# GpSimd only subtracts, ScalarE makes the first parts of its weight pieces, and two small chains of VectorE stand earlier

## The chip, the cores and the metric

The kernel runs on one core of a Trainium2 chip. Its time is the device time of one execution in microseconds (us), here the median of three. The engines of the core are named as in the profile: PE is TensorE (PEld its weight loads), DVE is VectorE, ACT is ScalarE, POOL is GpSimd, and SP issues the loads from HBM. Each engine works through its own list of instructions in order; they meet only in semaphores.

## The reference

Two transformer blocks run one after the other on 256 tokens of width 1024, all in float32. The second block is the one that the change touches: its input projection makes the queries, keys and values of a gated delta rule, of a compressed, a selected and a windowed attention, and the gates of both.

```
def first_block(...):           # three attentions, then a gated FFN
    h = h + concat([y_a, y_b, y_c]) @ w_out
    h = h + (silu(hn @ w_gate) * (hn @ w_up)) @ w_down
    return rms_norm(h, final_norm)[:, META_BLK:]

def second_block(x, ...):
    h = rmsnorm(x, norm_mix)
    (dn_qkv, dn_z, dn_b, dn_a, ns_q, ns_kc, ..., ns_gate, gate_dn, gate_nsa) = split(h @ w_in)
    o_dn = gated_deltanet(dn_qkv, dn_z, dn_b, dn_a, dn_conv, dn_a_log, dn_dt_bias, dn_out_norm)
    o_ns = nsa_mixer(...)
    mix = sigmoid(gate_dn) * (o_dn @ w_proj_dn) + sigmoid(gate_nsa) * (o_ns @ w_proj_nsa)
    x = x + mix @ w_out
    return x + square(relu(rmsnorm(x) @ w_up)) @ w_down

def gated_deltanet(qkv, z, b_logit, a_logit, ...):
    q, k, v = split(silu(causal_depthwise_conv(qkv, conv_w)))
    q, k = l2norm(q), l2norm(k)
    beta = sigmoid(b_logit)
    g = -exp(a_log) * softplus(a_logit + dt_bias)
    o = chunk_gated_delta_rule(q, k, v, g, beta)
    return rmsnorm(o, out_norm) * silu(z)
```

## The kernel before

**Weight pieces.** All weights come in some 250 pieces, most of 128 partitions by 1024 float32 numbers (512 KB), in the fixed order of the list `PIECES`. SP loads piece i into slot i modulo 5 of `raw`, as soon as the second part of piece i-5 is made. Each piece is then split into two parts of a faster matrix format, in slot i modulo 6 of `parts`: the first part is a rounded copy, the second is what is left (piece minus first part). A product on PE takes three matmuls: first by first, first by second, second by first (lines 529 to 531).

**Who splits.** For most pieces ACT makes the first part (`first_parts`, line 1302) and DVE the second (`second_parts`, line 1814). Twenty pieces, `dv1`, `dq0`, `dq1`, `z0` and `z1` (four each), are in `BY_POOL`: POOL makes both parts in `pool_parts`, a cast (line 1753) and a subtraction (line 1755). ACT and DVE come to their splits through `full`, `freed` and `beyond`: before they wait for a product of PE they split the four pieces that follow the ones that this product used. POOL has no such rule: it takes the next piece when it is loaded and the slot in `parts` is free.

**The join.** Where the second block's projections go over into its attention (`attention(G2, ...)`), each engine's order is written by hand. DVE does the four-tap convolutions of the keys (`convolve("k", 0, 4, 0)`, then `("k", 0, 4, 1)`, the jobs `cv_k2` and `cv_k3`) and of the first values (`EARLY`, the job `cv_v0`), each seven or eight reads of a PSUM bank and a last read (line 2213) that gives the bank back. Then it scales the residual X by its norm and gain (`inv_sqrt`, 11 dependent instructions in lines 1838 to 1846, and two of line 2265), makes the gates (lines 2268 to 2274), and takes the peaks of the first attention groups (`peaks_of`, line 1891). ACT makes exponentials from the peaks (line 1344), PE turns these (line 610 or 624).

**In the attention.** There are 24 groups (compressed, selected and windowed, each for four heads). Between them seven "fillers" stand at groups 0, 1, 3, 4, 7, 10 and 13 (`FILL`): PE makes a product of two pieces, DVE convolves it. Filler 0 uses `dv0.2` and `dv0.3`, filler 1 `dv1.0` and `dv1.1`, and so on to `dq1.3`. At groups 15, 17, 19 and 21 ACT makes decays (line 1613).

**After the attention.** POOL masks the four tiles of decays (line 1765) and scales them by the keys' norms (line 1772). ACT applies SiLU to the convolutions (line 1555). PE does the product of `z0`, turns, the products `qk` and `kk` (line 1120), and then the product of `z1`. The banks for the product of `z1` are the first two of `qk` and `kk`, which DVE gives back in lines 2404 and 2406, after it has made the queries' norms (`inv_rms`, lines 1838 to 1854).

Of the kernel before, what the change touches and what calls it, by code (L numbers as in the profile page):

```python
# [150 lines left out]
def build(nc, consts, params, weights, x, meta, out, line_dram):  # L151
    ctx = ExitStack()
    with ctx:
# [5 lines left out]
        def sem(name):  # L159
            if name not in sems:  # L160
                sems[name] = ctx.enter_context(nc.semaphore(name))
            return sems[name]
# [132 lines left out]
        def signal(ins, name, by=1):  # L295

            ins.then_inc(sem(name), by)
            counts[name] = counts.get(name, 0) + by
            return counts[name]
# [12 lines left out]
        def loaded(eng, name):  # L312

            i = INDEX[name]
            eng.wait_ge(sem(f"piece_in{i % RAW}"), 16 * (i // RAW + 1))
            return raw[:, i % RAW, 0:WIDTHS[name]]

        def split_slot(name):

            if name in APART:  # L320
                apart = arena_r[:, apart_at[APART.index(name)]:][:, 0:2 * PIECE]
                return apart[:, 0:PIECE], apart[:, PIECE:2 * PIECE]
            j = PART[name] % SPLIT
            return parts[:, j, 0, 0:WIDTHS[name]], parts[:, j, 1, 0:WIDTHS[name]]

        def slot_free(eng, name):

            if name not in APART and PART[name] >= SPLIT:
                used_up(eng, RING[PART[name] - SPLIT])
# [954 lines left out]
        def _(act):  # L1284
# [9 lines left out]
            def first_parts(n):  # L1294

                for name in PIECES[at[0]:n]:
                    at[0] += 1
                    if name in WHOLE or name in BY_POOL:
                        continue
                    whole_piece = loaded(act, name)  # L1300
                    slot_free(act, name)
                    signal(A(split_slot(name)[0], whole_piece, ACT.Copy), "first_parts")  # L1302

            keep_ahead[act] = first_parts

# [413 lines left out]
        @block.gpsimd  # L1719
        def _(pool):  # L1720
            nc.gpsimd.memset(ones[:, :], 1.0).then_inc(sem("ones"), 1)
            nc.gpsimd.memset(att1["PTm"], 0.0).then_inc(sem("meta_zero"), 1)
            nc.gpsimd.memset(one["V"][:, 0:768], 0.0).then_inc(sem("meta_zero"), 1)
            nc.gpsimd.memset(VC[:, :, :], 0.0).then_inc(sem("vc_zero"), 1)
            nc.gpsimd.memset(kcT[:, :, :], 0.0).then_inc(sem("kc_zero"), 1)

            pool.wait_ge(sem("lines_out"), 16)

            def shifted(head0, heads, v, m0, n):
                return bass.AP(tensor=line_dram.tensor, offset=head0 * 2 * LINE + v * LINE + m0,  # L1730
                               ap=[[1, P], [2 * LINE, heads], [1, n]])

            sz0 = one["sz0"].rearrange("p (h n) -> p h n", h=SH)
            sz1 = one["sz1"].rearrange("p (h n) -> p h n", h=SH)
            pool.dma_start(one["dz"].rearrange("p (h n) -> p h n", h=DH), shifted(0, DH, 0, 0, ALL)).then_inc(sem("dz_in"), 16)
            pool.dma_start(sz0[:, :, 0:META], shifted(DH, SH, 0, P, META)).then_inc(sem("sz_in"), 16)
            pool.dma_start(sz0[:, :, META:144], shifted(DH, SH, 1, P + META, P)).then_inc(sem("sz_in"), 16)
            pool.dma_start(sz1[:, :, 0:META], shifted(DH, SH, 0, 0, META)).then_inc(sem("sz_in"), 16)
            pool.dma_start(sz1[:, :, META:ALL], shifted(DH, SH, 1, META, SEQ)).then_inc(sem("sz_in"), 16)

            pool.wait_ge(sem("norm3"), 2)
            al = nsa["alibi"].rearrange("p (h n) -> p h n", h=NSH)
            for h in range(NSH):
                slope = float(np.float32(2.0 ** (-8.0 * (h + 1) / NSH)))
                nc.gpsimd.tensor_scalar(al[:, h, :], cst("negdist"), slope, None, ALU.mult).then_inc(sem("alibi"), 1)  # L1745

            def pool_parts(names):

                for name in names:
                    whole_piece = loaded(pool, name)  # L1750
                    slot_free(pool, name)
                    first, second = split_slot(name)
                    nc.gpsimd.tensor_copy(first, whole_piece).then_inc(sem("pool_first"), 1)
                    pool.wait_ge(sem("pool_first"), TURN[name])
                    nc.gpsimd.tensor_tensor(second, whole_piece, first.bitcast(F32), ALU.subtract)\  # L1755
                        .then_inc(sem("split_pool"), 1)

            by_pool = [name for name in PARTED if name in BY_POOL]
            pool_parts(by_pool[:-2])

            E4 = dn["DT"].rearrange("p (g n) -> p g n", g=4)
            for g in range(4):
                pool.wait_ge(sem("dec_exp"), g + 1)
                v = E4[:, g, :].rearrange("p (n i) -> p n i", n=GH)
                nc.gpsimd.tensor_tensor(v, v, cst("upper").unsqueeze(1).to_broadcast([P, GH, P]), ALU.mult)\
                    .then_inc(sem("dec_masked"), 1)
            pool.wait_ge(sem("key_scale"), 1)
            for g in range(4):
                pool.wait_ge(sem("dec_masked"), g + 1)
                v = E4[:, g, :].rearrange("p (n i) -> p n i", n=GH)  # L1770
                k2 = st[:, 112 + GH * g:116 + GH * g].unsqueeze(2).to_broadcast([P, GH, P])
                nc.gpsimd.tensor_tensor(v, v, k2, ALU.mult).then_inc(sem("dec_scaled"), 1)
            pool_parts(by_pool[-2:])

            pool.wait_ge(sem("split_pool"), len(by_pool))
            pool.wait_ge(sem("y_new"), 1)
            nc.gpsimd.memset(dn["Yi"].rearrange("p (g n) -> p g n", g=2 * GH * TT)[HB:P, :, 0:HB], 0.0).then_inc(sem("y_zero"), 1)

            for j in range(FT2 // 2):
                v = relu2[:, j % 4, :]  # L1780
                pool.wait_ge(sem("hidden2_first"), j + 1)
                nc.gpsimd.tensor_tensor(v, v, v, ALU.mult).then_inc(sem("squares2"), 1)  # L1782
                pool.wait_ge(sem("squares2"), j + 1)
                nc.gpsimd.tensor_tensor(a2[:, 1, 2 * j:2 * j + 2, :], v, a2[:, 0, 2 * j:2 * j + 2, :].bitcast(F32), ALU.subtract)\
                    .then_inc(sem("hidden2"), 1)
# [3 lines left out]
        def _(dve):  # L1789
# [403 lines left out]
            def convolve(which, w, first, n):  # L2193

                name = f"cv_{which}{first // 2 + n}"
                full(dve, name)
                both = [(first + 2 * n + j, bank_of(name)[:, SEQ * j:SEQ * j + SEQ]) for j in range(2)]
                for h, raw in both:
                    step(V_.tensor_scalar(cv[:, w, h, :], raw, taps[:, 8 * w + h, 3:4], None, ALU.mult))
                settle()  # L2200
                for back in (1, 2, 3):
                    for h, raw in both:
                        o = cv[:, w, h, back:SEQ]
                        ins = V_.scalar_tensor_tensor(out=o, in0=raw[:, 0:SEQ - back], scalar=taps[:, 8 * w + h, 3 - back:4 - back],
                                                      in1=o, op0=ALU.mult, op1=ALU.add)
                        if back < 3:
                            step(ins)
                        else:
                            signal(ins, "conv_raw")
                    if back < 3:  # L2210
                        settle()

                release(V_.tensor_copy(scr[:, 512 + n:513 + n], bank_of(name)[:, 0:1]), name)  # L2213
# [42 lines left out]
            for t in range(TT):  # L2256
                v = nsa["ksw"][:, 512 * t:512 * t + 512].rearrange("p (h d) -> p h d", d=ND)
                signal(V_.tensor_tensor(v, v, bc(st[:, 80 + 8 * t:88 + 8 * t], [P, 8, ND]), ALU.mult), "nk_norm")
            convolve("k", 0, 4, 0)
            convolve("k", 0, 4, 1)  # L2260
            for what in EARLY:
                convolve(*what)
            inv_sqrt(st[:, 4:6], st[:, 30:32], st[:, 0:2], st[:, 24:26])
            for t in range(TT):
                signal(V_.scalar_tensor_tensor(out=X[:, t, :], in0=X[:, t, :], scalar=st[:, 4 + t:5 + t], in1=att1["final"],
                                               op0=ALU.mult, op1=ALU.mult), "x2")
            dve.wait_ge(sem("small_ln"), 1)
            link(V_.tensor_scalar(sig[:, :], sig[:, :], 1.0, None, ALU.add))
            link(V_.reciprocal(sig[:, :], sig[:, :]))
# [3 lines left out]
            link(V_.tensor_scalar(soft[:, 48:56], soft[:, 48:56], -1.0, None, ALU.mult))  # L2273
            signal(V_.tensor_tensor(gl[:, :, :], soft[:, 0:16].rearrange("p (t h) -> p t h", t=TT),
                                    soft[:, 48:56].unsqueeze(1).to_broadcast([P, TT, NH2]), ALU.mult), "gates")

            def finish_two(g):

                c0 = g["first"]
# [401 lines left out]
```

## Time and profile before

| what | value |
|---|---|
| median of 3 runs | 962.51 us (961.49 to 962.91) |
| the profiled execution's own time | 962.28 us |
| its span, first to last instruction | 960.4 us |
| PE busy | 915.4 us, 95% |
| DVE busy | 630.2 us, 66% |
| ACT busy | 465.3 us, 48% |
| POOL busy | 156.2 us, 16% |
| PE idle at the join | 13.1 us, in one wait |
| mean granted clock of PE | 0.991 |

A profile row has its start in us, how long it took, the engine, the line of the kernel, the instruction, and what it writes and reads. "x4" joins four alike in a row. In brackets stands how long the engine was idle just before, and who released it. PEclk is the clock granted to PE as a share of 2.4 GHz, so 0.50 is 1.2 GHz.

### The profile page before, as it was taken

How to read it: one execution, taken by the hardware profiler on the slowest of the kernel's cores; microseconds unless marked ns; L12 is line 12 of the kernel's file. 1: busy time of each engine (PE TensorE's matmuls, PEld its weight loads, DVE VectorE, ACT ScalarE, POOL GpSimd, SP SyncE). 2: the span in 40 equal slices, each digit the busy share in tenths (PEclk: the TensorE clock that was granted, in tenths of full speed). 3: DMA queues.
4: the chain of work that ended last, by engine and by line, in shares of the span. 5: the costliest groups of instructions: out<-in, count | busy, mean ns of one | idle time of the engine just before them, and what ended most of it. 6: DMA issues, size and time to landing. Idle time of an engine off the chain costs nothing. (4 is left out here: it accounts for less than half of the span.)

```text
span 960.4 us, 17495 instructions
## 1 busy us (share of the span) xinstructions
PE 915.4 (95%) x6858; PEld 818.7 (85%) x6858; DVE 630.2 (66%) x1338; ACT 465.3 (48%) x925; POOL 156.2 (16%) x111
## 2 busy tenths in 40 slices
PE   4999899999999999999499999999999999999998
PEld 1988687999999989889488898898888889999996
DVE  4556776656556678697787977545966666445543
ACT  6554555545344463564134575354454454454441
POOL 2000000000000015005475314000000023233221
PEclk9999999999999999999799999999999999999999
DMA  8530244565556445646232202022455546555551
GB/s 303 177 135 23 88 133 130 158 216 182 171 195 220 155 143 176 219 160 203 77 114 86 67 1 78 3 70 88 164 187 178 186 153 218 186 176 176 184 189 44
DMA packets 38679, 139.61 MB, mean 145 GB/s; under 512 B 4331, under 2 KB 4587, under 8 KB 38597
## 3 DMA queue, kind: packets, MB, share of 16 engines
q1 hardware_dynamic: 37184, 134.17, 42.3%
q10 hardware_dynamic: 884, 2.49, 0.8%
q0 software_dynamic: 528, 1.84, 0.6%
q8 instruction: 55, 0.90, 0.4%
q14 instruction: 28, 0.22, 0.1%
HBM read 137.39 MB, written 1.08 MB: 144 GB/s over the span
## 5 line engine op out<-in xcount | busy, mean ns | idle before, releaser
L1814 DVE TENSOR_TENSOR parts<-raw,parts 128x1024 fp32r<-128x1024 f32 (+2 forms) x225 | 286.8, 1310 | 138.6 <-ACT parts L1302 134.1
L1302 ACT ACTIVATE parts<-raw 128x1024 fp32r<-128x1024 f32 (+2 forms) x225 | 228.0, 1050 | 119.2 <-PE psum L531 97.7
L529 PE MATMUL psum<-hT,parts 128*128 128x256 f32 (+1 forms) x928 | 264.7, 285 | 2.3 <-DVE hT L1831 2.0
L530 PE MATMUL psum<-hT,parts 128*128 128x256 f32 (+1 forms) x928 | 263.4, 284 | 0.0
L531 PE MATMUL psum<-hT,parts 128*128 128x256 f32 (+1 forms) x928 | 261.7, 282 | 0.0
L529 PEld LDWEIGHTS psum<-hT,parts 128*128 128x128 f32 x928 | 175.7, 189 | 5.6 <-DVE hT L1831 2.9
L531 PEld LDWEIGHTS psum<-hT,parts 128*128 128x128 f32 x928 | 176.9, 191 | 0.0
L530 PEld LDWEIGHTS psum<-hT,parts 128*128 128x128 f32 x928 | 176.0, 190 | 0.6
L529 PE MATMUL psum<-parts,arena_r 128*128 128x512 f32 x344 | 135.1, 393 | 0.9 <-DVE arena_r L1829 0.7
L531 PE MATMUL psum<-parts,arena_r 128*128 128x512 f32 x344 | 134.0, 389 | 0.0
L530 PE MATMUL psum<-parts,arena_r 128*128 128x512 f32 x344 | 133.9, 389 | 0.0
L1344 ACT ACTIVATE arena<-arena,npeaks 128x128 f32<-128x128 f32 (+4 forms) x136 | 55.9, 414 | 66.5 <-DVE npeaks L1913 51.3
L529 PEld LDWEIGHTS psum<-parts,arena_r 128*128 128x128 f32 x344 | 64.6, 188 | 14.6 <-DVE arena_r L1829 1.8
L531 PEld LDWEIGHTS psum<-parts,arena_r 128*128 128x128 f32 x344 | 64.6, 188 | 13.6
L530 PEld LDWEIGHTS psum<-parts,arena_r 128*128 128x128 f32 x344 | 64.6, 188 | 12.6
L529 PE MATMUL psum<-parts,hT 128*128 128x512 f32 (+1 forms) x176 | 69.7, 396 | 1.7 <-DVE peaks L1891 1.1
L1745 POOL TENSOR_SCALAR arena<-cbuf 128x256 f32<-128x256 f32 x16 | 16.8, 1050 | 333.8 <-DVE scr L2131 332.7
L530 PE MATMUL psum<-parts,hT 128*128 128x512 f32 (+1 forms) x176 | 68.8, 391 | 0.0
L531 PE MATMUL psum<-parts,hT 128*128 128x512 f32 (+1 forms) x176 | 68.7, 390 | 0.0
L1782 POOL TENSOR_TENSOR arena<-arena 128x512 f32<-128x512 f32 x16 | 17.2, 1075 | 284.7 <-ACT arena_r L1715 284.7
L1755 POOL TENSOR_TENSOR parts<-raw,parts 128x1024 fp32r<-128x1024 f32 x20 | 48.4, 2418 | 1.6
L652 PE MATMUL psum<-arena 128*128 128x128 f32 x288 | 40.2, 276 | 2.1 <-DVE scr L2213 1.2
(324 smaller groups left out, 1184.5 us busy)
## 6 DMA issues: line engine op xcount, KB each, us to landing
raw<-weights SPq DMA_DIRECT2D x247, 512.0 KB, 4.1
raw<-weights SPq DMA_DIRECT2D x4, 384.0 KB, 7.4
X<-x SPq DMA_DIRECT2D x2, 512.0 KB, 6.1
out<-X SPq DMA_DIRECT2D x2, 512.0 KB, 2.6
arena<-lines POOLq DMA_DIRECT2D x1, 768.0 KB, 9.7
cbuf<-consts ACTq DMA_DIRECT2D x1, 561.0 KB, 5.1
arena<-lines POOLq DMA_DIRECT2D x1, 544.0 KB, 7.8
arena<-params ACTq DMA_DIRECT2D x1, 512.0 KB, 8.9
```

Of the source, the lines that this page charges most:

```text
L529: mm(ps, a, c, start=start, stop=False)
L530: mm(ps, a, d, start=False, stop=False)
L531: return mm(ps, b, c, start=False, stop=stop)
L652: last = mm(o, flat[:, at:at + P], vt[t], start=(t == 0 and not g["meta"]), stop=(t == g["tiles"] - 1))
L1302: signal(A(split_slot(name)[0], whole_piece, ACT.Copy), "first_parts")
L1344: signal(A(map_slot(g, E, n), map_slot(g, S, n), ACT.Exp, bias=npeaks[:, col:col + 1], accum_out=sums[:, col:col + 1]), tag)
L1745: nc.gpsimd.tensor_scalar(al[:, h, :], cst("negdist"), slope, None, ALU.mult).then_inc(sem("alibi"), 1)
L1755: nc.gpsimd.tensor_tensor(second, whole_piece, first.bitcast(F32), ALU.subtract)\
L1782: nc.gpsimd.tensor_tensor(v, v, v, ALU.mult).then_inc(sem("squares2"), 1)
L1814: signal(V_.tensor_tensor(second, whole_piece, first.bitcast(F32), ALU.subtract), "split_vector")
```

## The change

Three things change.

POOL's cast is gone. For the twenty pieces of `BY_POOL`, ACT now makes the first part too, in its usual `first_parts`, and signals `first_for_pool`; POOL waits for that and only subtracts. ACT's place for it is that of every other piece: up to four pieces ahead of the last product that it has come to.

The gates (five instructions) move ahead of the convolution `cv_k2`.

The residual's norm and scaling (13 instructions) move ahead of the convolution `cv_k3`, behind an explicit call that makes the second parts due there.

```diff
                 for name in PIECES[at[0]:n]:
                     at[0] += 1
-                    if name in WHOLE or name in BY_POOL:
+                    if name in WHOLE:
                         continue
                     whole_piece = loaded(act, name)
                     slot_free(act, name)
-                    signal(A(split_slot(name)[0], whole_piece, ACT.Copy), "first_parts")
+                    signal(A(split_slot(name)[0], whole_piece, ACT.Copy), "first_for_pool" if name in BY_POOL else "first_parts")
...
             def pool_parts(names):
 
                 for name in names:
+                    first, second = split_slot(name)
+                    pool.wait_ge(sem("first_for_pool"), TURN[name])
                     whole_piece = loaded(pool, name)
-                    slot_free(pool, name)
-                    first, second = split_slot(name)
-                    nc.gpsimd.tensor_copy(first, whole_piece).then_inc(sem("pool_first"), 1)
-                    pool.wait_ge(sem("pool_first"), TURN[name])
                     nc.gpsimd.tensor_tensor(second, whole_piece, first.bitcast(F32), ALU.subtract)\
                         .then_inc(sem("split_pool"), 1)
...
-            convolve("k", 0, 4, 0)
-            convolve("k", 0, 4, 1)
-            for what in EARLY:
-                convolve(*what)
-            inv_sqrt(st[:, 4:6], st[:, 30:32], st[:, 0:2], st[:, 24:26])
-            for t in range(TT):
-                signal(V_.scalar_tensor_tensor(out=X[:, t, :], in0=X[:, t, :], scalar=st[:, 4 + t:5 + t], in1=att1["final"],
-                                               op0=ALU.mult, op1=ALU.mult), "x2")
             dve.wait_ge(sem("small_ln"), 1)
             link(V_.tensor_scalar(sig[:, :], sig[:, :], 1.0, None, ALU.add))
             link(V_.reciprocal(sig[:, :], sig[:, :]))
...
+            convolve("k", 0, 4, 0)
+            second_parts(beyond("cv_k3"))
+            inv_sqrt(st[:, 4:6], st[:, 30:32], st[:, 0:2], st[:, 24:26])
+            for t in range(TT):
+                signal(V_.scalar_tensor_tensor(out=X[:, t, :], in0=X[:, t, :], scalar=st[:, 4 + t:5 + t], in1=att1["final"],
+                                               op0=ALU.mult, op1=ALU.mult), "x2")
+            convolve("k", 0, 4, 1)
+            for what in EARLY:
+                convolve(*what)
```

ACT, start of the second block's attention. Line 1302 is a first part, 1344 the exponentials, 1362 and 1370 copies of turned probabilities. Before:

```order
 L1344 ACTIVATE arena,sums<-arena,npeaks 128x15 x4
 L1344 ACTIVATE arena,sums<-arena,npeaks 128x128 x4
-L1362 ACTIVATE arena<-psum 128x128
-L1344 ACTIVATE arena,sums<-arena,npeaks 128x128 x4
-L1370 ACTIVATE arena<-psum 128x512
```

And in the changed kernel at the same place:

```order
+L1302 ACTIVATE parts<-raw 128x1024 x4
+L1362 ACTIVATE arena<-psum 128x128
+L1344 ACTIVATE arena,sums<-arena,npeaks 128x128 x4
+L1302 ACTIVATE parts<-raw 128x1024 x2
+L1370 ACTIVATE arena<-psum 128x512
```

Four first parts (`dv1.0` to `dv1.3`) now stand behind the exponentials of the first two groups, and two more behind the next ones; pairs follow with fillers 2 to 6, sixteen in all.

ACT after the attention. Line 1555 is SiLU, 1562 takes the product of `z0` out of PSUM:

```order
 L1555 ACT_TABLE_LOAD
 L1555 ACTIVATE arena<-arena 128x512 x8
-L1302 ACTIVATE parts<-raw 128x1024
+L1302 ACTIVATE parts<-raw 128x1024 x5
 L1562 ACTIVATE arena<-psum 128x512 x2
 L1302 ACTIVATE parts<-raw 128x1024
```

The first parts of `z1.0` to `z1.3` now come behind all eight SiLU instructions, ahead of that of `gn0.0`.

POOL, the same stretch, of the changed kernel. Lines 1753 are subtractions (`dv1.0` to `z1.1`, then `z1.2` and `z1.3`), 1763 the masks of the decays, 1770 their scaling:

```order
+L1753 TENSOR_TENSOR parts<-raw,parts 128x1024 x18
+L1763 TENSOR_TENSOR arena<-arena,cbuf 128x512 x4
+L1770 TENSOR_TENSOR arena<-arena,st 128x512 x4
+L1753 TENSOR_TENSOR parts<-raw,parts 128x1024 x2
```

POOL's order is as before but for the casts: the subtractions of `z1.0` and `z1.1` stand ahead of the masks, those of `z1.2` and `z1.3` behind the scaling.

DVE at the join, of the changed kernel. Line 1812 is a second part, 2197 to 2211 a convolution, 1836 to 1844 the norm (its middle left out below), 2270 the scaling of X:

```order
477 L2264 TENSOR_TENSOR gl<-soft 128x16
478 L1812 TENSOR_TENSOR parts<-raw,parts 128x1024 x2
479 L2197 TENSOR_SCALAR arena<-psum,pbuf 128x256 x2
...
483 L2211 COPY scr<-psum 128x1
484 L1812 TENSOR_TENSOR parts<-raw,parts 128x1024 x6
485 L1836 TENSOR_SCALAR st<-st 128x2
...
496 L2270 SCALAR_TENSOR_TENSOR X<-X,st,arena 128x1024 x2
497 L2197 TENSOR_SCALAR arena<-psum,pbuf 128x256 x2
```

The gates now end ahead of `cv_k2`; the norm and the scaling stand between the six second parts and the convolution `cv_k3`, where before `cv_k3` came directly behind the six.

## Rows read from the trace of the kernel before

**Rows 1.** The page's clock line, and PE's longest wait: us in total, times, longest.
```profile
PEclk9999999999999999999799999999999999999999
...
PE psum L610 <- ACT arena L1344: 13.1, 1, 13.1
```

**Rows 2.** Timeline of PE around the join: start, us, line, operation, idle before.
```profile
452.08 0.38 PE L529 MATMUL psum<-hT,parts 128*128 128x256 f32 x1 [0.28 <-DVE scr L2213]
...
471.17 0.47 PE L610 MATMUL psum<-cbuf,arena 128*128 128x128 f32 x1 [13.13 <-ACT arena L1344]
...
480.25 0.28 PE L531 MATMUL psum<-hT,parts 128*128 128x256 f32 x1
```

**Rows 3.** Timeline of DVE at the join.
```profile
433.64 4.62 DVE L1814 TENSOR_TENSOR parts<-raw,parts 128x1024 fp32r<-128x1024 f32 x4
443.74 4.71 DVE L1814 TENSOR_TENSOR parts<-raw,parts 128x1024 fp32r<-128x1024 f32 x2 [5.49 <-ACT parts L1302]
448.38 0.86 DVE L2199 TENSOR_SCALAR arena<-psum,pbuf 128x256 f32<-128x256 f32 x2
...
455.51 2.13 DVE L1838 TENSOR_SCALAR st<-st 128x2 int32<-128x2 int32 x1
...
465.06 2.48 DVE L2265 SCALAR_TENSOR_TENSOR X<-X,st,arena 128x1024 f32<-128x1024 f32 x2
467.46 0.21 DVE L2268 TENSOR_SCALAR sig<-sig 128x112 f32<-128x112 f32 x1
...
469.10 0.17 DVE L1891 CUSTOM_DVE_ANT_0 arena<-psum,cbuf 128x15 f32<-128x15 f32 x1
```

**Rows 4.** Timeline of POOL beside DVE's row at 455.51.
```profile
455.22 2.40 POOL L1755 TENSOR_TENSOR parts<-raw,parts 128x1024 fp32r<-128x1024 f32 x1
```

**Rows 5.** Timeline of ACT: first exponentials, and the copy behind two groups of them.
```profile
469.85 0.31 ACT L1344 ACTIVATE arena<-arena,npeaks 128x15 f32<-128x15 f32 x1 [15.86 <-DVE npeaks L1913]
...
472.56 0.25 ACT L1362 ACTIVATE arena<-psum 128x128 f32<-128x128 f32 x1
```

**Rows 6.** Windows: us, busy PE, PEld, DVE, ACT, POOL, then PEclk, DMA share, GB/s.
```profile
50.00:53.50 3.50, 3.50 (x14) 3.50 (x13) 2.42 (x13) 3.50 (x17) 0.00 (x0) 0.53 0.70 256
...
471.00:477.00 6.00, 5.83 (x29) 5.38 (x30) 4.92 (x27) 3.36 (x19) 0.00 (x0) 0.51 0.00 0
```

**Rows 7.** Timeline of PE: the wait ahead of the first of those windows.
```profile
49.43 0.41 PE L529 MATMUL psum<-parts,hT 128*128 128x384 f32 x1 [1.06 <-DVE peaks L1891]
```

**Rows 8.** Timeline of DVE in the attention's last filler.
```profile
536.49 1.68 DVE L1913 TENSOR_SCALAR npeaks<-peaks 128x4 f32<-128x4 f32 x1
```

**Rows 9.** Timeline of PE, its wait behind that filler.
```profile
541.87 0.35 PE L652 MATMUL psum<-arena 128*128 128x128 f32 x1 [1.18 <-DVE scr L2213]
```

**Rows 10.** Timeline of ACT after the attention.
```profile
579.35 4.28 ACT L1555 ACTIVATE arena<-arena 128x512 f32<-128x512 f32 x8
585.69 1.06 ACT L1302 ACTIVATE parts<-raw 128x1024 fp32r<-128x1024 f32 x1 [2.07 <-PE psum L531]
```

**Rows 11.** Timeline of POOL: masks and scaling of the decays, the last subtraction.
```profile
551.81 1.27 POOL L1765 TENSOR_TENSOR arena<-arena,cbuf 128x512 f32<-128x512 f32 x1 [10.26 <-ACT arena L1613]
...
583.35 4.04 POOL L1772 TENSOR_TENSOR arena<-arena,st 128x512 f32<-128x512 f32 x4 [9.90 <-DVE st L2368]
...
592.89 2.35 POOL L1755 TENSOR_TENSOR parts<-raw,parts 128x1024 fp32r<-128x1024 f32 x1
```

**Rows 12.** The page's line on the weight loads: KB each, us from issue to landing.
```profile
raw<-weights SPq DMA_DIRECT2D x247, 512.0 KB, 4.1
```

**Rows 13.** Timeline of DVE: the queries' norms and what follows them.
```profile
592.80 2.29 DVE L2382 TENSOR_REDUCE st<-arena 128x16 f32<-128x2048 f32 x1 [1.46 <-ACT arena L1644]
595.12 0.18 DVE L1854 TENSOR_SCALAR st<-st 128x16 f32<-128x16 f32 x1
...
597.71 0.69 DVE L2404 TENSOR_TENSOR arena<-psum,arena 128x512 f32<-128x512 f32 x1
```

**Rows 14.** Timeline of PE: the product of z1 begins.
```profile
599.10 0.47 PE L529 MATMUL psum<-parts,hT 128*128 128x512 f32 x1
```

## The prediction

> **What bounds the kernel now.** The page's shares come first: PE is busy nearly all the time, so the time is PE's work plus its waits. The list of PE's waits and the clock line show where PE is not at its best. One wait of 13.1 us stands at the join of the second block's projections and its attention, and the clock line has its only 7 there [rows 1]. The other long wait, at the start, is not touched. The timeline of PE then gives the wait's ends: PE finishes filler 0 at 471.17 - 13.13 = 458.04 and comes back at 471.17 [rows 2]. ACT had waited 15.86 for peaks [rows 5], and DVE's timeline shows why [rows 3]: behind two convolutions it began the residual's norm at 455.51, reached the gates at 467.46 and the first peaks only at 469.10. Eleven tiny instructions of the norm took 465.06 - 455.51 = 9.55 us. The first of them took 2.13 and ended with the POOL subtraction that had started ahead of it, 455.22 + 2.40 = 457.62 [rows 3, 4]. So the join is bound by DVE, and DVE by POOL. After the wait PE runs at the lower clock until 477 [rows 6].
>
> **The join, after the change.** I walk the queues from the last common point, and keep the before kernel's clock times.
>
> Gates: 469.10 - 467.46 = 1.64 us, now ahead of `cv_k2`. They fit in the 5.49 us in which DVE waited for ACT ahead of 443.74 [rows 3], so they cost nothing. Were that cover gone they would cost their 1.64 again.
>
> Second parts: the last two still start at 443.74, but POOL has no piece yet (below), so each takes 4.62 / 4 = 1.16 instead of 4.71 / 2 [rows 3]. They end at 446.05.
>
> Norm: 13 such instructions without POOL take 597.71 - 595.12 = 2.59 [rows 13], 11 take 2.2. The scaling takes 467.46 - 465.06 = 2.40 [rows 3]. DVE is at 450.65.
>
> Convolutions: two took 455.51 - 448.38 = 7.13, each 3.56 [rows 3]. `cv_k3` ends at 454.2. PE's filler 0 needs its bank: it began at 452.08, released by that convolution's last read [rows 2]. Now it begins 454.3, a new wait of 2.2 us, and ends 458.04 - 452.08 = 5.96 later, at 460.25. `cv_v0` ends at 457.8, the first peaks follow, ACT's exponentials 469.85 - 469.10 = 0.75 later [rows 3, 5] at 458.5, PE could go on at 471.17 - 469.10 = 2.07 behind the peaks, at 459.9. So PE does not wait for exponentials any more: the wait of 13.1 is gone.
>
> What is late next is filler 1. It needs `dv1.0`, which POOL had long made before. Now ACT's first part of `dv1.0` stands behind two groups of exponentials: 458.5 + (472.56 - 469.85 = 2.71) = 461.2 [rows 5], plus 1.06 [rows 10] is 462.3. POOL's subtraction (2.40) ends at 464.7 [rows 4]. PE has turned group 0 and made scores by 461.2 and waits about 3.5 us. The next subtraction ends at 467.1, in time for the second half at 467.8. Filler 1 ends at 464.8 + 5.96 = 470.8, before it ended at 480.25 + 0.28 = 480.53 [rows 2]: a gain of 9.7.
>
> Clock: the before kernel had the lower level, 0.51, until 477 [rows 6], and that is in its 480.53. A wait of 1.06 at 49.43 was enough for some 3 us of 0.53 [rows 6, 7], so the two new waits probably bring that. At half the clock 3 us cost 1.5. The bounds are 0, and the whole of the 6 us of the second window, 3.0. I take 1.5, the shorter row. The join gains 8.2 (6.7 to 9.7).
>
> ACT's four first parts (4.2 us) also stand ahead of the copy for group 0, which PE needs only behind filler 1, so they are hidden. POOL's slots and loads: `dq0.1` is loaded when `dv1.0` is split, 464.7 + 4.1 = 468.8 [rows 12], and ACT waits for it ahead of a copy that PE asks for at 470.8. Hidden, by 1 us.
>
> **In the attention.** Sixteen more first parts on ACT are 17 us, in pairs of 2.1, and each pair falls in filler time in which ACT waits for PE. POOL loses 20 casts. What can change is when POOL blocks DVE. At the last filler a peak instruction took 1.68 instead of about 0.17 and PE waited 1.18 for the convolution behind it [rows 8, 9]. By my walk POOL subtracts there during the convolution, which reads PSUM, so 0.8 is gained, and small blocks of 0.2 at two more. Against that, behind filler 2 POOL's pairs of subtractions come close on each other, DVE's small SBUF instructions are held by up to two of them (4.8 less what runs meanwhile), and by my walk its convolution of filler 3 starts 1.6 late. Together 0 (between -1.5 and +2.5).
>
> **After the attention.** Here stands the price. POOL's list has the masks of the decays behind the subtractions of `z1.0` and `z1.1`. ACT makes those first parts only behind its eight SiLU. POOL, which masked at 551.81 and three times later [rows 11], now does nothing until ACT is at 579.35 + 4.28 = 583.63 plus one first part, 584.7 [rows 10]. Then its list is: two subtractions 4.7 (2.35 each), four masks 4 x 1.27 = 5.1, the scaling 4.04, two subtractions 4.7: 18.5 us [rows 11], to which DVE's one second part (1.16) comes. It is busy until about 604.4, where before it ended at 592.89 + 2.35 = 595.24, just as DVE began the queries' norms at 595.12 [rows 11, 13].
>
> DVE's start of that norm moves too: the first part of `gn0.1` needs the slot of `z1.0`, split at 587.1, landed at 591.2 by the median [rows 12] (PE's next squares wait behind it on ACT), so DVE's sum (592.80, 2.29) ends near 596.3 instead of 595.1 [rows 13]. Six POOL instructions are still to come. At the join eleven such instructions took 9.55 us beside POOL, 0.87 each [rows 3]. At that pace ten of thirteen are done when POOL, itself made a little later by those let in, ends near 605; the last three go at 0.2 each. DVE reaches line 2404 at about 605.8 to 606 instead of 597.71. PE's product of `z1` began 599.10 - 597.71 = 1.39 behind that [rows 13, 14], while PE had just ended the work before it, so there is no slack: 8.3 us of new wait. The lower bound is 1.2, if only the later sum counts and POOL holds nothing. The upper is 9.5, POOL's whole list and one instruction at a time. I take 8.3, since the join's rows are the same instructions against the same subtractions.
>
> That wait is long enough to lower the clock: 1.5 by the shorter row (0 to 3.0) [rows 6].
>
> The Trainium skill, SBUF — State Buffer, section "SBUF: two separate sides", says the pair of ports that DVE and GpSimd share is a lock held for a whole instruction, and the loser waits. The 2.13 us for a 128x2 instruction agree [rows 3]. By that rule the wait here stays near 8; if the two shared bandwidth instead, thirteen tiny instructions would hardly lengthen and the sum would lie with the first rival.
>
> **The sum.** 962.28 is the profiled execution's own time (its span is 960.4, and 1.9 lies around it; it stands 0.2 under the median of the runs). 962.28 - 8.2 + 0 + 8.3 + 1.5 = 963.9, or 964.1 against the median. Two of the terms are at the unkind end of where they could be (the wait behind the masks and the clock), so I put the forecast at 963.4: the join's gain is given back behind the attention. Its own range is 960 to 966.5.
>
> **The rivals.**
> First, the hold-up after the attention costs little: DVE gets in between POOL's instructions, or starts its norm ahead of the scaling, and the wait is 1.2 to 4. For it: at the join not all eleven instructions were held, since 9.55 us is less than eleven waits of 2.13. Against it: 9.55 is still four times their own 2.2, and POOL's list here is 18.5 us long [rows 3, 11]. The time is 962.3 - 9.7 + 2.5 = 955.1, up to 958 with a clock loss of 1.5 at each end. Chance 0.31.
> Second, slower: POOL's subtractions block DVE inside the attention as well. Place: between fillers 2 and 6, where each pair (4.8 us) starts when ACT has made the first parts rather than when a slot is free, and can fall on the two or three SBUF instructions that stand ahead of each convolution. Price: up to 1.6 at each of five fillers, with the waits above. It decides from the point where DVE starts a convolution later than PE ends its filler, since the bank is given back by it (0.28 at 452.08) [rows 2]. Five times 1.2 on the sum is 969. For it: the 1.68 row [rows 8]. Against it: ACT's first parts mostly fall into the filler itself. Chance 0.25.
> Third, the change does not do what it says at the join: ACT's parts come so late that filler 1 waits as long as the old wait. Against it: ACT has nothing else to do after its exponentials, and POOL needs one subtraction. Gain 3 instead of 8.2: 963.4 + 5.2 = 968.6. Chance 0.07.
> The forecast has 0.37.
>
> **How the numbers follow.** This measurement can tell 0.2%, 1.9 us, from no change: 960.6 to 964.4. The forecast's 0.37 divides into 0.07 under, 0.20 within and 0.10 over, by its own range. The first rival is under, but for 0.02 within. The second has 0.03 within and 0.22 over, the third is over. Faster is 0.07 + 0.29 = 0.36, same 0.20 + 0.02 + 0.03 = 0.25, slower 0.10 + 0.22 + 0.07 = 0.39. The range 955 to 969 holds about 8 in 10.
>
> **What would show it.** The join: PE's wait for line 610 gone, filler 0 beginning near 454.3, a wait of 3 to 4 for POOL's first subtraction ahead of filler 1, that filler ended near 471. The norm of the residual in about 2.2. After the attention: no mask before ACT's SiLU are done, POOL busy some 19 us on end, the queries' norm taking over 7 us rather than 2.6, and a wait of PE of about 8 ahead of the product of `z1`, with a low clock behind it. Wrong would be: a wait there under 3, or new waits of over 1 us at each filler.

## The result, and the profile after

The changed kernel takes 965.16 us (median of 8 runs, 962.08 to 966.35), the kernel before 962.14 (8 runs on the same chip, 960.74 to 963.26). The ratio is 1.0028, with a 95% interval of 1.0018 to 1.0039: the change makes the kernel 0.3% slower. The forecast was 963.4 in a range of 955 to 969. The profiled execution took 965.20 us, 2.9 more than that of before (962.28); its span is 963.4 and its mean granted clock 0.988.

The list of PE's waits in the kernel after (us in total, times, longest) tells the story in four lines. The wait for line 610 [rows 1] is gone, the first three below have come (the third was one of 0.3), and the fourth has grown from 1.0 in all:

```profile
PE psum L529 <- DVE arena L2402: 7.8, 1, 7.8
PE psum L529 <- POOL parts L1753: 3.8, 1, 3.8
PE psum L529 <- DVE scr L2211: 2.4, 1, 2.4
PE psum L594 <- DVE scr L2211: 2.1, 3, 1.5
```

**The join.** The timeline of DVE answers to [rows 3]: the norm begins at 445.34, while POOL is silent, and its eleven small instructions take 447.37 - 445.34 = 2.03 us, not 9.55.

```profile
445.34 0.16 DVE L1836 TENSOR_SCALAR st<-st 128x2 int32<-128x2 int32 x1
...
447.17 0.16 DVE L1844 SCALAR_TENSOR_TENSOR st<-st 128x2 f32<-128x2 f32 x1
447.37 2.48 DVE L2270 SCALAR_TENSOR_TENSOR X<-X,st,arena 128x1024 f32<-128x1024 f32 x2
449.77 0.87 DVE L2197 TENSOR_SCALAR arena<-psum,pbuf 128x256 f32<-128x256 f32 x2
```

The timeline of PE answers to [rows 2]: filler 0 waits 2.36 for `cv_k3`, line 610 no longer waits, filler 1 waits 3.82 for POOL's first subtraction, and its last matmul ends at 471.93 + 0.28 = 472.21, 8.3 us before the 480.53 of [rows 2].

```profile
453.48 0.39 PE L529 MATMUL psum<-hT,parts 128*128 128x256 f32 x1 [2.36 <-DVE scr L2211]
...
459.28 0.27 PE L610 MATMUL psum<-cbuf,arena 128*128 128x128 f32 x1
...
464.01 0.55 PE L529 MATMUL psum<-hT,parts 128*128 128x256 f32 x1 [3.82 <-POOL parts L1753]
...
471.93 0.28 PE L531 MATMUL psum<-hT,parts 128*128 128x256 f32 x1
```

Filler 1 lasts 8.20 us, not the 5.96 of a filler at the full clock. The windows say why (us, busy PE, PEld, DVE, ACT, POOL, then PEclk, DMA share, GB/s): the granted clock is 0.58 in the 6 us from 464, behind the wait.

```profile
464.00:470.00 6.00, 5.99 (x31) 6.00 (x32) 2.23 (x1) 3.97 (x12) 6.00 (x3) 0.58 0.63 186
470.00:476.00 6.00, 5.66 (x49) 4.90 (x47) 3.64 (x10) 2.33 (x10) 5.54 (x3) 1.00 0.75 248
```

**In the attention** the product of `z0` starts at 569.64, before at 577.00: 7.36 of the 8.32 us are left. PE's new wait of 1.45 at 494.98 stands behind filler 3. There POOL had four subtractions on end, from 480.87 to 490.33, and DVE's two small instructions on SBUF ahead of the convolution took 1.59 and 2.12 (DVE, then PE):

```profile
486.40 1.59 DVE L2286 TENSOR_TENSOR st<-st,sig 128x4 f32<-128x4 f32 x1
...
488.49 2.12 DVE L2305 TENSOR_TENSOR arena<-arena,scr 128x256 f32<-128x256 f32 x1
```

```profile
494.98 0.71 PE L594 MATMUL psum<-arena 64*128 64x128 f32 x6 [1.45 <-DVE scr L2211]
```

**After the attention.** POOL had stood idle for 42 us, since its next piece needs ACT. Then it has no gap from 577.29 to 591.92 + 4.63 = 596.55: two subtractions, four masks, four scalings, two subtractions. This answers to [rows 11].

```profile
577.29 4.76 POOL L1753 TENSOR_TENSOR parts<-raw,parts 128x1024 fp32r<-128x1024 f32 x2 [42.23 <-ACT parts L1302]
582.01 5.96 POOL L1763 TENSOR_TENSOR arena<-arena,cbuf 128x512 f32<-128x512 f32 x4
587.93 4.03 POOL L1770 TENSOR_TENSOR arena<-arena,st 128x512 f32<-128x512 f32 x4
591.92 4.63 POOL L1753 TENSOR_TENSOR parts<-raw,parts 128x1024 fp32r<-128x1024 f32 x2
```

The timeline of DVE in the same stretch, which answers to [rows 13]. Read it beside the four rows above. Each dependent instruction of 128x16, 0.17 us when alone, ends when a POOL instruction does: about 1 us each beside the scalings of 1 us, 2.26 each beside the subtractions of 2.3. From 596.62, with POOL idle, all take 0.17 again.

```profile
586.26 2.29 DVE L2380 TENSOR_REDUCE st<-arena 128x16 f32<-128x2048 f32 x1 [0.73 <-ACT arena L1644]
588.58 0.42 DVE L1852 TENSOR_SCALAR st<-st 128x16 f32<-128x16 f32 x1
589.03 0.96 DVE L1836 TENSOR_SCALAR st<-st 128x16 int32<-128x16 int32 x1
589.91 1.08 DVE L1837 TENSOR_SCALAR st<-st 128x16 f32<-128x16 f32 x1
591.03 0.96 DVE L1842 TENSOR_TENSOR st<-st 128x16 f32<-128x16 f32 x1
592.03 2.26 DVE L1843 TENSOR_TENSOR st<-st 128x16 f32<-128x16 f32 x1
594.33 2.26 DVE L1844 SCALAR_TENSOR_TENSOR st<-st 128x16 f32<-128x16 f32 x1
596.62 0.17 DVE L1842 TENSOR_TENSOR st<-st 128x16 f32<-128x16 f32 x1
...
598.09 0.69 DVE L2402 TENSOR_TENSOR arena<-psum,arena 128x512 f32<-128x512 f32 x1
```

The norm takes 598.09 - 588.58 = 9.5 us, not 2.59, and PE waits 7.81. The two rows of PE (the first answers to [rows 14]) stand at both ends of the product of `z1`. Its last matmul ends at 613.69, so it takes 14.2 us, before 610.51 - 599.10 = 11.4, and the window behind the wait shows a clock of 0.50.

```profile
599.48 0.77 PE L529 MATMUL psum<-parts,hT 128*128 128x512 f32 x1 [7.81 <-DVE arena L2402]
...
613.62 0.56 PE L1138 MATMUL psum<-cbuf,arena 64*64 64x64 f32 x12
```

```profile
600.00:604.00 4.00, 4.00 (x11) 3.08 (x10) 3.77 (x9) 0.00 (x0) 0.95 (x1) 0.50 0.13 52
```

Line 1138 began at 610.44 before, at 613.62 now: 3.2 us late, which accounts for the whole difference of the spans (963.4 - 960.4 = 3.0).

### The profile page after: what moved, and what is told of

The parts are those of the page before. It is cut to its first block and busy times, and to the rows that moved or that the text cites. A ratio compares the mean times of both kernels' runs of the same rounds, so it can differ in the third digit from the quotient of the medians.

```text
span 963.4 us, 17510 instructions
## 1 busy us (share of the span) xinstructions
PE 919.7 (95%) x6858; PEld 821.6 (85%) x6858; DVE 626.9 (65%) x1338; ACT 484.3 (50%) x945; POOL 133.3 (14%) x91
## 5 line engine op out<-in xcount | busy, mean ns | idle before, releaser
L1812 DVE TENSOR_TENSOR parts<-raw,parts 128x1024 fp32r<-128x1024 f32 (+2 forms) x225 | 284.8, 1302 | 138.0 <-ACT parts L1302 131.1
L1302 ACT ACTIVATE parts<-raw 128x1024 fp32r<-128x1024 f32 (+2 forms) x245 | 247.8, 1049 | 128.7 <-PE psum L531 102.4
L529 PEld LDWEIGHTS psum<-parts,hT 128*128 128x128 f32 x176 | 33.7, 192 | 17.3 <-DVE arena L2402 8.0
```

What stands on the lines that cost most here:

```text
L529: mm(ps, a, c, start=start, stop=False)
L1812: signal(V_.tensor_tensor(second, whole_piece, first.bitcast(F32), ALU.subtract), "split_vector")
```

## The experiments

The kernel before was timed beside each. Its median was 961.2 us beside the first four and 962.1 beside the last four, so the kernels are best compared by their ratios to it. The kernel after stands at 1.0028.

**The moves alone.** The norm and the gates are moved as in the change, and POOL makes both parts of its pieces as before:

```diff
                 for name in names:
-                    pool.wait_ge(sem("first_for_pool"), TURN[name])
                     whole_piece = loaded(pool, name)
...
+                    nc.gpsimd.tensor_copy(first, whole_piece)   # the cast of before
...
                     nc.gpsimd.tensor_tensor(second, whole_piece, first.bitcast(F32), ALU.subtract)
```

> The kernel before with only DVE's two moves (gates, residual norm); POOL keeps its cast and its own pace. If DVE's small instructions are held by POOL (the theory), the norm now stands in the middle of POOL's run (441 to 464), takes some 9 us again, and the convolution cv_k3 behind it gives its bank to filler 0 about 9 us later than in the changed kernel, near 462. The wait at the join is then moved ahead of filler 0 and not removed: 960 to 966, within 0.4% of before. The rival is that the order alone gave the join's gain (gates and norm off the path): then the join is as short as in the changed kernel, with nothing lost behind the attention, and the time is 953 to 955.

Measured: 962.57 us (960.22 to 963.55), ratio 1.0007 (0.9998 to 1.0016). The wait has only changed its name. Filler 0 of PE now waits as long as line 610 did:

```profile
464.57 0.58 PE L529 MATMUL psum<-hT,parts 128*128 128x256 f32 x1 [12.81 <-DVE scr L2213]
```

The timelines of DVE (first fence) and POOL (second) show the norm beside POOL's casts and subtractions: it lasts from 448.70 to 458.46, 9.8 us. A small instruction issued inside a subtraction ends with it (452.26 + 2.19 = 454.45, 452.09 + 2.34 = 454.43).

```profile
448.70 2.35 DVE L1838 TENSOR_SCALAR st<-st 128x2 int32<-128x2 int32 x1
450.96 0.15 DVE L1839 TENSOR_SCALAR st<-st 128x2 f32<-128x2 f32 x1
451.15 0.88 DVE L1844 TENSOR_TENSOR st<-st 128x2 f32<-128x2 f32 x1
452.06 0.16 DVE L1845 TENSOR_TENSOR st<-st 128x2 f32<-128x2 f32 x1
452.26 2.19 DVE L1846 SCALAR_TENSOR_TENSOR st<-st 128x2 f32<-128x2 f32 x1
```

```profile
447.78 3.24 POOL L1755 TENSOR_TENSOR parts<-raw,parts 128x1024 fp32r<-128x1024 f32 x1
450.97 1.04 POOL L1753 CAST parts<-raw 128x1024 fp32r<-128x1024 f32 x1
452.09 2.34 POOL L1755 TENSOR_TENSOR parts<-raw,parts 128x1024 fp32r<-128x1024 f32 x1
```

What follows: the place of the norm is worth little while POOL works beside it (filler 1 ends at 479.19, 1.3 us earlier than before, and the kernel is no faster).

**The split alone.** POOL only subtracts, as in the change; norm and gates stay where they were.

```diff
-            ...                        # the gates
             convolve("k", 0, 4, 0)
-            second_parts(beyond("cv_k3"))
-            inv_sqrt(...)              # and the two scalings
             convolve("k", 0, 4, 1)
             for what in EARLY:
                 convolve(*what)
+            inv_sqrt(...)              # and the two scalings, then the gates
```

> The kernel before with only the other part: ACT makes the first parts, POOL subtracts, DVE's order as before. Theory: the norm at the join takes 2.2 us instead of 9.55 and the last two second parts 2.36 instead of 4.71, so the first peaks come at about 459.5 and filler 1, which waits for POOL, begins near 466; no wait ahead of filler 0. The loss behind the attention (wait near 7.8, product of z1 at the lower clock for some us) is all there. 965 to 968, 0 to 3 us above the changed kernel. Rival: if the moves carried the gain, the join stays as before and the loss adds: 971 to 973.

Measured: 967.59 us (965.42 to 968.25), ratio 1.0057 (1.0045 to 1.0070). The wait for line 610 shrinks to 4.3, POOL's parts hold filler 1 for 3.4, filler 1 ends at 474.84 (5.7 us earlier than before), and PE's wait ahead of the product of `z1` is 7.8, as in the kernel after. So both sides of the account, most of the join's gain and the loss behind the attention, belong to the change of POOL and ACT. The moves add 474.84 - 472.21 = 2.6 us to the gain, but 0.9 of that was there ahead of the join already, where the matmul of line 1030 ends at 439.09 here and at 438.18 in the kernel after. That leaves 1.7.

**The first parts of z1 early.** The kernel after, with one line in ACT's list, inside the attention ahead of the first decay:

```diff
             def decay_exponents():
+                first_parts(INDEX["z1.1"] + 1)
                 act.wait_ge(sem("gc_out"), 1)
```

> The changed kernel with one line more: ACT makes the first parts of z1.0 and z1.1 in the attention, ahead of the decays of group 15, so POOL has them split before its masks. Theory (POOL's late list holds DVE's norm of the queries): masks on time, POOL done with scaling and its last two subtractions before that norm, norm near 2.6 us, the wait of 7.8 ahead of the product of z1 gone and its low clock (14.2 instead of 11.4 us) too: 965.2 - 7.8 - 2.8 = 954.6, 953.5 to 956.5. Rival (the twenty first parts cost ACT its place in the attention and behind it, and the wait comes from ACT): two more first parts in the attention make that worse or leave it, 962 to 966.

Measured: 956.49 us (955.46 to 956.99), ratio 0.9944 (0.9932 to 0.9957). POOL's subtractions of `z1.0` and `z1.1` now end inside the attention, its masks come as the decays do, and its list of 18.5 us behind the attention is broken up:

```profile
544.79 4.68 POOL L1754 TENSOR_TENSOR parts<-raw,parts 128x1024 fp32r<-128x1024 f32 x2 [9.62 <-ACT parts L1302]
549.42 1.28 POOL L1764 TENSOR_TENSOR arena<-arena,cbuf 128x512 f32<-128x512 f32 x1
...
566.18 1.27 POOL L1764 TENSOR_TENSOR arena<-arena,cbuf 128x512 f32<-128x512 f32 x1 [6.37 <-ACT arena L1614]
577.35 4.04 POOL L1771 TENSOR_TENSOR arena<-arena,st 128x512 f32<-128x512 f32 x4 [9.90 <-DVE st L2367]
581.34 5.68 POOL L1754 TENSOR_TENSOR parts<-raw,parts 128x1024 fp32r<-128x1024 f32 x2
```

PE no longer waits ahead of the product of `z1`, and that takes 11.4 us again. The price is 1.35 us in the attention (the product of `z0` starts at 570.99, not 569.64), where PE waits 1.0 for exponentials. ACT's two copies are not all of that: ahead of these exponentials ACT itself waits 1.61 for peaks of DVE, of whose instructions one, at 558.62, took 1.21 beside a mask of POOL. The run does not tell the two apart. The sum, 7.8 + 2.8 - 1.35 = 9.3 us, stands against 963.4 - 954.7 = 8.7 between the spans.

**The masks first.** The kernel after, but POOL does the four masks ahead of the subtractions of `z1.0` and `z1.1`, and ACT is unchanged:

```diff
-            pool_parts(by_pool[:-2])
+            pool_parts(by_pool[:-4])
             ...                        # the four masks
+            pool_parts(by_pool[-4:-2])
             pool.wait_ge(sem("key_scale"), 1)
```

> The changed kernel with POOL's masks of the decays ahead of the subtractions of z1.0 and z1.1; ACT's order untouched, so ACT's five first parts in a row, its squares and the late load of gn0.1 stay. Theory: POOL's run behind ACT's SiLU is shorter by the masks (5.96), it ends near 591 instead of 596.5, one or two of DVE's thirteen norm instructions are held instead of six, DVE gives the banks 4 to 5 us earlier, the wait is near 3 with a clock loss of 0 to 3: 957.5 to 961. Rival (the wait comes from ACT and the load): no change, 964 to 966.

Measured: 960.14 us (958.53 to 960.96), ratio 0.9986 (0.9977 to 0.9995). POOL's list behind the attention is 5 us shorter (from 577.12 to 591.48). Two of the norm's instructions are still held (0.89 and 2.27), the wait is 3.58, and the product takes 13.0 us: half of the loss is back.

**The scaling in sixteen pieces.** The kernel after, with the same elements in more instructions:

```diff
-                nc.gpsimd.tensor_tensor(v, v, k2, ALU.mult).then_inc(sem("dec_scaled"), 1)
+                for n in range(GH):
+                    nc.gpsimd.tensor_tensor(v[:, n:n + 1, :], v[:, n:n + 1, :], k2[:, n:n + 1, :], ALU.mult)\
+                        .then_inc(sem("dec_scaled"), 1)
```

> The kernel after with GpSimd's four scalings of 128x512 cut into sixteen of 128x128: the same elements, and some 1 us more in all for GpSimd. It tells how GpSimd holds VectorE. Theory (a small dependent instruction of VectorE gets its turn between two GpSimd instructions, one for one): the twelve dependent instructions of the queries' norm behind the reduction find sixteen gaps instead of six, are through about when the scaling is, at some 593 us, and the wait of 7.8 us ahead of the product of z1 shrinks to 1 to 3 us, with part of the 2.8 us of low clock in the product; the time is 957 to 960 us. Rival (VectorE is held in proportion to the time for which GpSimd is at the memory, whatever the length of its instructions): the norm ends as late as before, with the scaling's added time on top, and the time is 965 to 967 us.

Measured: 959.49 us (957.99 to 960.50), ratio 0.9973 (0.9962 to 0.9983): 0.55% below the kernel after, though POOL works 1.7 us longer on the scaling. The timeline of POOL and then that of DVE:

```profile
588.39 5.75 POOL L1771 TENSOR_TENSOR arena<-arena,st 128x128 f32<-128x128 f32 x16
594.10 5.13 POOL L1753 TENSOR_TENSOR parts<-raw,parts 128x1024 fp32r<-128x1024 f32 x2
```

```profile
589.10 0.43 DVE L1854 TENSOR_SCALAR st<-st 128x16 f32<-128x16 f32 x1
...
590.28 0.32 DVE L1844 TENSOR_TENSOR st<-st 128x16 f32<-128x16 f32 x1
590.64 0.32 DVE L1845 TENSOR_TENSOR st<-st 128x16 f32<-128x16 f32 x1
590.99 0.32 DVE L1846 SCALAR_TENSOR_TENSOR st<-st 128x16 f32<-128x16 f32 x1
```

DVE's steps come every 0.36 us, and POOL's too (5.75 / 16). One gets its turn for one of the other's. The norm, ahead of line 2404, ends at 593.85, and PE's wait is 3.1. This decides between a hold for whole instructions and a share of the bandwidth: with a share the norm would have ended later, not 4.2 us earlier.

**The first parts of dv1 early.** The kernel with the early first parts of `z1` (ratio 0.9944), and besides ACT makes those of `dv1.0` and `dv1.1` between its SiLU of the keys:

```diff
                 conv_pieces(w, first, half)
+                if (w, first, half) == (0, 4, 1):
+                    act.wait_ge(sem("x2"), 2)
+                    first_parts(INDEX["dv1.1"] + 1)
```

> The kernel after with the first parts of z1.0 and z1.1 made in the attention (as in the run that took 956.5 us), and the first parts of dv1.0 and dv1.1 made by ScalarE between its convolutions, as soon as the norm's sum of squares is known, so that GpSimd subtracts them while VectorE is still at the convolutions. Theory (the 3.8 us wait of TensorE at the second filler of the join is for GpSimd's late subtractions alone, and the low clock behind it is its consequence): the wait goes, with 1 to 2 us of the clock behind it, so 956.5 - 3.8 - 1 to 2 = 950.7 to 951.7 us, range 949 to 953. Rival (GpSimd's work only moves from one stretch to another, and holds VectorE's convolutions or its peaks of the first groups instead): the filler gets its parts, but another wait of 2 to 4 us stands elsewhere in the join, and the time stays at 955 to 958.

Measured: 951.41 us (949.60 to 952.33), ratio 0.9887 (0.9871 to 0.9902). POOL subtracts at 451.86, while DVE convolves out of PSUM and isn't held. Filler 1 goes without a wait at 462.47 and takes 5.96 us at the full clock. Filler 0, still 2.35 late, takes 7.5.

**The norm in the gap.** The same, and DVE takes fewer second parts ahead of the norm, so that this falls into the 3.8 us in which it waited for ACT:

```diff
-            second_parts(beyond("cv_k3"))
+            second_parts(INDEX["dv0.1"] + 1)
```

> The run before it in this list, and besides VectorE takes only its own pieces up to dv0.1 ahead of the residual's norm, not those up to cv_k3: the norm then stands where VectorE sat idle for 3.8 us until ScalarE had its parts. Theory (the norm's 4.5 us stand in the path of filler 0's second parts, and fill the idle time if they come earlier): filler 0's wait of 2.4 us goes, and 950.7 to 951.7 us become 948 to 950, range 947 to 951. Rival (the norm's small instructions now stand beside GpSimd's subtractions of the same stretch, one held for each of them): the norm takes 6 to 10 us, filler 0 waits as long as before or longer, and the time is that of the run before it or 1 to 3 us more.

Measured: 946.89 us (946.39 to 948.49), ratio 0.9849 (0.9835 to 0.9862). That is better than its expected 948 to 950 and just under the whole range (947). The expectation had counted filler 0's wait of 2.4 alone; with the wait the filler's low clock went too. Filler 0 starts at 451.33 without a wait and takes 5.95 us, not 7.5; filler 1 ends at 463.93, and no window of the join that I read is below the full clock:

```profile
451.00:457.00 6.00, 6.00 (x55) 5.88 (x52) 5.03 (x34) 3.51 (x18) 0.00 (x0) 1.00 0.38 125
458.00:464.00 6.00, 6.00 (x53) 6.00 (x52) 4.68 (x18) 4.53 (x12) 5.94 (x3) 1.00 0.36 95
```

**Another place for the first parts of z1.** The same, but ACT makes them right behind the attention, in the 2.9 us in which it waits for PE, and POOL masks ahead of their subtractions:

```diff
             attention(G2, extra)
+            first_parts(INDEX["z1.1"] + 1)
```

> The run before it in this list, but the first parts of z1.0 and z1.1 are made behind the attention, in the 2.9 us in which ScalarE waits for TensorE, and GpSimd does its four masks ahead of their subtractions. Theory (the attention lost 1.3 us to the two ScalarE copies and to GpSimd's two subtractions in it; behind it GpSimd has room for both before the scaling): the product of z0 starts 1.3 us earlier, GpSimd is through before the queries' norm begins, and the time is 0.5 to 1.5 us below that of the run before it. Rival (the two subtractions, 4.7 us long, now stand beside the keys' norm on VectorE and hold it, so that the scaling starts late): the wait ahead of the product of z1 comes back with 1 to 4 us, and the time is 0 to 3 us above that of the run before it.

Measured: 946.88 us (945.68 to 947.49), ratio 0.9844 (0.9831 to 0.9857): no difference from the run before that these intervals could show. Both mechanisms of the expectation came true, and in the traces they nearly cancel. The product of `z0` starts 1.57 us earlier, 0.3 of it from ahead of the join. But POOL's two subtractions (first fence) hold two of DVE's instructions for the attention's last output (second), so the keys' norm and all behind it come later, and a wait of 1.1 is back ahead of the product of `z1` (third).

```profile
556.60 4.90 POOL L1756 TENSOR_TENSOR parts<-raw,parts 128x1024 fp32r<-128x1024 f32 x2 [0.64 <-ACT parts L1302]
```

```profile
556.78 2.47 DVE L2309 TENSOR_TENSOR arena<-arena,scr 128x256 f32<-128x256 f32 x1
...
559.50 2.03 DVE L2290 TENSOR_TENSOR st<-st,sig 128x4 f32<-128x4 f32 x1
```

```profile
582.60 0.47 PE L529 MATMUL psum<-parts,hT 128*128 128x512 f32 x1 [1.07 <-DVE arena L2406]
```

The hold was not at the keys' norm, where the rival had put it, but one step ahead of it. The last two kernels are the fastest of this study, 1.5% below the kernel before, and they keep every part of the change.

## Why the prediction was right, and where it was off

The sum of the prediction was 963.9, the profiled execution 965.2, or 1.3 more. In the trace the terms add up as follows, in us against the kernel before at the start of line 1138. Ahead of the join the execution is 0.7 earlier already (the matmul of line 1030 that ends PE's work there ends at 438.18, before at 438.85; in the other kernels of this study it ends between 438.1 and 439.3, also in three whose code is that of the kernel after up to there, so I take it for chance).

| term | predicted | measured |
|---|---|---|
| ahead of the join | 0 | -0.7 |
| join without the clock | -9.7 | -9.9 |
| clock at the join | +1.5 | +2.2 |
| attention | 0 | +1.0 |
| wait ahead of the product of `z1` | +8.3 | +7.7 |
| clock behind it | +1.5 | +2.8 |
| sum | +1.6 | +3.2 |

The measured terms are rounded singly; unrounded they add up to 3.18.

**The join**, right in its mechanism and its size. Moved by the 0.7 of the head start, filler 0 begins at 454.2 (predicted 454.3), and filler 1 at 464.7 behind a wait of 3.8 (464.8 and 3.5). The gates cost nothing. The norm took 2.03, against 2.2. The two single edits show what was not written in the prediction. From the end of line 1030 to the end of filler 1 the kernel before takes 41.7 us, the moves alone 40.4, the silent POOL alone 35.8, both 34.0.

**The attention**, mis-sized within its bounds (0, with -1.5 to +2.5). The gain at the last filler came, 1.18 - 0.45 = 0.7, with 0.8 predicted. The loss at filler 3, for which the prediction had a convolution 1.6 late, came with 1.2, and it is larger on PE than I had allowed for. From the start of filler 3 to the end of filler 4 PE lost 2.2 us: the wait is 1.1 longer, and behind it the clock is low again (0.79 in the window from 493 to 501), so that the matmuls of lines 652 and 594 take 1.75 and 1.23 us, not 1.13 and 0.71, and filler 4 takes 6.35, not 5.96; a wait of 0.58 is gone. The sum put the clock there at nothing. The second rival, five such delays, had its mechanism at one filler only (its five times 1.2 on 963.4 is 969.4, not 969).

**The wait ahead of the product of z1**, right. POOL's masks came only behind ACT's SiLU; POOL was busy 19.3 us on end (predicted 18.5 and one second part of DVE); the norm took 9.5 us; PE waited 7.8. The two rearrangements and the cut in sixteen each took away POOL's part in it, and the wait shrank to nothing, 3.6 and 3.1. The pace of 0.87 us per instruction, taken from the join, was not a constant, as the cut shows: it is the length of whatever POOL instruction stands beside. Six of the thirteen were held, for 596.62 - 588.58 = 8.0 us, where the prediction had ten in 8.7. That the pace gave about the right sum is luck: the mix of 1 and 2.3 us here is like that of casts and subtractions there.

**The clock**, the term that was mis-sized. The prediction put 1.5 us behind each of the two long waits, by the shorter of two rows (3 us of 0.53), against an upper bound of 3.0 by the longer. Measured are 2.2 behind 3.8 us and 2.8 behind 7.8 us: the row of 6 us was the nearer one. Together that is 2.0 more than predicted (5.0 against 3.0); all other terms together are 0.5 less. For a wait of 2.4 us, at filler 0, the prediction had no separate term. In the kernel after this filler takes 5.96 us, and so it does with the first parts of z1 early. With the same wait in three other kernels (the masks first, the scaling in sixteen, dv1 early) it takes 7.5. The first two of these have the code of the kernel after up to there, so the difference is not one of code; what makes it stays open. In them PE then waits 2.3 for POOL, not 3.8, and filler 1 takes 7.4, not 8.2: it ends 33.3 us behind line 1030, not 34.0. So the 2.2 us of the clock at the join are those of one execution, and in such a comparison of two single traces 0.8 us can come from this.

**The choice of 963.4** instead of the 963.9 of the sum went the wrong way: one of the two terms named as unkind, the clock, was not unkind enough.

## What to carry to other kernels

When work leaves an engine, write down what is left in its queue, when each item can now start, and which other engine it holds up there: this change made POOL's work on each piece shorter and its start later, and its backlog then fell on a chain of tiny DVE instructions just where PE waited for that chain. Beside POOL instructions back to back such a chain cost one of them per link; so keep POOL silent there by giving it its inputs earlier (0.84% here), or cut its instructions small (0.55%). A stall can cost more than its length: behind the waits of 3.8 and 7.8 us the product ran partly at the lower clock and lost another 2.2 and 2.8. Look for gaps that can be filled by reordering alone, as the norm did that moved into one of 3.8 us (0.38%).

## What the runs showed that I had not expected

- The hold is one for one: steps of 0.36 us beside POOL instructions of 0.36, 1.0 beside 1.0, 2.3 beside 2.3. POOL in its turn is held by DVE: the four masks take 5.96 us on end in the kernel after, and 1.27 each where they stand apart [rows 11]. The excess is in the first of them (2.27), which begins beside a second part of DVE that ends at 583.13.
- Not every DVE instruction is held. The reduction of 128x2048 from SBUF took 2.29 us at 586.26 in the kernel after, beside POOL's masks and first scaling, and 2.29 with the norm in the gap at 562.26, where POOL was silent. Six steps of a convolution, which read one tensor from PSUM and one from SBUF, took 2.68 us beside POOL (449.27 in the kernel before) and with POOL silent (450.67 in the kernel after). The Trainium skill, SBUF — State Buffer, section "SBUF: two separate sides", gives the lock to DVE's faster modes and to instructions with two SBUF inputs; these rows agree with it.
- Where POOL has a gap of its own, between a cast and the subtraction that needs it, one more small instruction slips through unheld (452.06 in the moves alone, 0.16 us, between the cast's end at 452.01 and the subtraction's start at 452.09). One did at a change from a subtraction to a cast too (450.96, 0.15 us). From 589.03 to 596.59 in the kernel after, beside instructions of POOL that do not wait for each other, none did.
- A cut that adds 1.7 us of POOL time made the kernel 5 us faster (0.55%).
